# Hybrid decoder step on one core: the first norm by token rows, key steps of whole pages, the feed-forward norm at the gate

## What is computed

```python
xn = rms_norm(x, norm_mix)                                  # x * rsqrt(mean(x*x) + eps) * gain
q_m,k_m,v_m,o_m,if_pre,q_a,k_a,v_a,g_m,g_a = split(xn @ w_in)
h_m = mlstm_chunkwise(...)                                  # 8 heads of 128, gates from if_pre
h_a = moba_attention(...)                                   # sample rows read 8 pages of 128 cached keys and values
x = x + (sigmoid(g_m) * (h_m @ w_proj_m) + sigmoid(g_a) * (h_a @ w_proj_a)) @ w_out
x = x + cross_attend(rms_norm(x, norm_xattn), memory)  # ends in @ w_xo
xf = rms_norm(x, norm_ffn)
x = x + (silu(xf @ w_ffn_gate) * (xf @ w_ffn_up)) @ w_ffn_down      # 5632 wide
y = rms_norm(x, norm_final)
```

## Time and profile before

| | us |
|---|---|
| median of 3 runs | 2252.89 |
| lowest to highest | 2250.77 to 2255.76 |
| the profiled execution | 2252.39 |
| its span | 2250.8 |
| PE busy in the span | 2122.3 |
| DVE busy | 1206.2 |
| ACT busy | 797.4 |
| POOL busy | 63.5 |

### The profile page before, as it was taken

One profiled execution on the slowest core, in us unless ns is written; L12 is line 12 of the kernel. 1 busy time (PEld: TensorE's weight loads), 2 busy tenths in 40 slices (PEclk: granted clock), 3 DMA queues, 4 the chain that ended last, 5 costly groups with the idle time before them and its releaser, 6 DMA issues.

```text
span 2250.8 us, 40554 instructions
## 1 busy us (share of the span) xinstructions
PE 2122.3 (94%) x16438; PEld 2001.4 (89%) x16438; DVE 1206.2 (54%) x1424; ACT 797.4 (35%) x1010; POOL 63.5 (3%) x85
## 2 busy tenths in 40 slices
PE   4999998999899999999999787999999999999997
PEld 3999897899677878999998666999999999999997
DVE  3354565343555646667455446666654466566444
ACT  3333342243333333333344323333333333333333
POOL 0001011111000000000000000000000000000000
PEclk8899997999999999999999988999999999999998
DMA  7146434445588687556444351545445554554553
GB/s 247 38 150 189 131 98 157 132 152 175 169 287 309 242 307 272 158 174 216 167 141 159 131 187 59 165 154 181 149 141 173 172 182 154 164 172 138 173 159 114
DMA packets 305493, 384.82 MB, mean 171 GB/s; under 512 B 6146, under 2 KB 278690, under 8 KB 304626
## 3 DMA queue, kind: packets, MB, share of 16 engines
q1 hardware_dynamic: 300530, 365.72, 49.4%
q0 software_dynamic: 4896, 18.13, 2.5%
HBM read 370.94 MB, written 12.88 MB: 171 GB/s over the span
## 4 chain that ended last, share of the span: by engine, by line
PE 89%; DVE 5%; ACT 2%; issue 1%; SPq 1%; DMA 1%; POOL 0%; PEldq 0%; DVEq 0%; PEld 0%; ACTq 0%; POOLq 0%
PE bank L1713 19%; PE bank L1714 19%; PE bank L1717 18%; PE bank L1727 8%; PE bank L1731 6%; PE bank L2174 4%; PE bank L2173 4%; PE bank L2178 4%; PE bank L1724 1%; PE bank L1953 1%; PE bank L1952 1%; PE bank L1956 1%; DVE w_lo L1051 1%; DVE n_tmp L1083 1%; ACT w_hi L639 1%
## 5 line engine op out<-in xcount | busy, mean ns | idle before, releaser
L1051 DVE TENSOR_TENSOR w_lo<-raw,w_hi 128x2048 fp32r<-128x2048 f32 (+2 forms) x289 | 604.8, 2096 | 584.5 <-ACT w_hi L639 580.1
L1713 PE MATMUL bank<-xn_hi,w_hi 128*128 128x288 f32 x3152 | 875.0, 304 | 45.0 <-DVE xn_lo L1091 26.0
L1714 PE MATMUL bank<-xn_lo,w_hi 128*128 128x288 f32 x3152 | 867.0, 301 | 0.0
L639 ACT ACTIVATE w_hi<-raw 128x2048 fp32r<-128x2048 f32 (+2 forms) x289 | 504.2, 1746 | 687.3 <-PE bank L1717 471.8
L1713 PEld LDWEIGHTS bank<-xn_hi,w_hi 128*128 128x128 f32 x3152 | 608.4, 193 | 58.3 <-issue 41.6
L1714 PEld LDWEIGHTS bank<-xn_lo,w_hi 128*128 128x128 f32 x3152 | 608.3, 193 | 0.1
L1717 PE MATMUL bank<-xn_hi,w_lo 128*128 128x288 f32 x3152 | 450.7, 295 | 0.0
L1717 PEld LDWEIGHTS bank<-xn_hi,w_lo 128*128 128x128 f32 x3152 | 430.1, 189 | 0.0
L2173 PE MATMUL bank<-f_hi,w_hi 128*128 128x288 f32 x704 | 191.4, 296 | 0.0
L2174 PE MATMUL bank<-f_lo,w_hi 128*128 128x288 f32 x704 | 190.8, 297 | 0.0
L2173 PEld LDWEIGHTS bank<-f_hi,w_hi 128*128 128x128 f32 x704 | 132.5, 188 | 0.1
(11 more groups left out here) (363 smaller groups left out, 1764.6 us busy)
## 6 DMA issues: line engine op xcount, KB each, us to landing
raw<-w_in_dram SPq DMA_DIRECT2D x44, 2048.0 KB, 8.6
raw<-w_ffn_gate_dram SPq DMA_DIRECT2D x22, 2048.0 KB, 8.0
raw<-w_ffn_up_dram SPq DMA_DIRECT2D x22, 2048.0 KB, 8.0
raw<-w_ffn_down_dram SPq DMA_DIRECT2D x32, 1408.0 KB, 6.4
raw<-cache_k_dram SPq DMA_DIRECT2D x64, 512.0 KB, 5.3
raw<-cache_v_dram SPq DMA_DIRECT2D x64, 512.0 KB, 5.2
raw<-w_out_dram SPq DMA_DIRECT2D x8, 2048.0 KB, 8.1
w_pm_raw<-w_proj_m_dram SPq DMA_DIRECT2D x8, 1024.0 KB, 5.1
```

The costliest lines, as they stand in the source:

```text
L639: nc.scalar.activation(like(wh[ph.half(c)], src), src, ACT.Copy).then_inc(hi_ready, 1)
L1051: nc.vector.tensor_tensor(like(wl[ph.half(c)], src), src, like(wh[ph.half(c)], src).bitcast(F32), ALU.subtract).then_inc(slot_read[ph.slot ...
L1713: mm(out, wh[half][:, k, :], rh[:, k, 0:n], start=k == 0, stop=False)
L1714: mm(out, wh[half][:, k, :], rl[:, k, 0:n], start=False, stop=False)
```

## The change

Three parts.

1. The head. SP loads x into buffers of its own (`xrow0`, `xrow1`), the parameters are loaded from ACT's queue, and the main projection's first weights follow the gate weights at once. The sums of squares are taken from the rows as loaded, one token a partition: the first 128 tokens and the 32 sample tokens by ACT (a square with a running sum), the other 128 by DVE. The root then has three columns. It is put on the diagonals of three matrices (`xdiag`), and PE multiplies each block of rows by them instead of transposing: the product is the transposed block, already scaled. ACT takes it with the gain as the high half, DVE the low half, block by block through six banks, and the gate tile's products follow five blocks behind (`gate_k`). The plain transposes for `xT` and the gate steps go between the eight tiles of the first pass (`first_step`), and so does everything that copies them.
2. Key steps are whole pages: eight transposes into two banks, ACT copies one and DVE the other, then eight scores of the page before. Two pairs of buffers are used in turn (`KTb`, `KTb2`). The copy of the last batch's rows (`rows_in`) goes ahead of the pages.
3. The feed-forward norm. As each block of x is added up, ACT and DVE split x times gain, with no root. POOL squares the blocks and adds them into `fsum`; PE sums over features behind the first gate tile. The root is applied where the gate is read: DVE multiplies the gate tile by it on its way out of PSUM (`up_scale`), ACT takes the exponential of that, and after the sigmoid DVE multiplies by the root once more, for the up half.

Semaphores of the last norm are merged into one. The core of the diff:

```diff
@@ SP
+            xp = a["x_prompt"].rearrange("b (t p) d -> (b t) p d", p=P)
+            for t in range(2):
+                sp.dma_start(xrow0[:, t, :], xp[t]).then_inc(x_in[t], 16)
+                if not t:
+                    sp.dma_start(blob[:], a["blob"]).then_inc(const_in, 16)
+            sp.dma_start(xrow1[:], a["x_sample"].rearrange("b t d -> (b t) d")).then_inc(x_in[2], 16)
...
-            for n, name in enumerate(("norm_mix", "norm_xattn", "norm_mem", "norm_ffn")):
-                sp.dma_start(grow[16 * n:16 * n + 16, :], a[name].rearrange("l (k p) -> (l k) p", p=P)).then_inc(params_in, 16)
...
-            sp.wait_ge(m_zero, 1)
-            for t in range(TS):
-                sp.dma_start(m0tok[t:NS:TS, 2, :], a["state_m"][0]).then_inc(params_in, 16)
@@ POOL
+            for m in range(KT):
+                gp.wait_ge(c_xo, m + 1)
+                pc.run(nc.gpsimd.tensor_tensor(fsq[:, m % 2, :] if m else fsum[:], xT[:, m, :], xT[:, m, :], ALU.mult))
+                if m:
+                    pc.sync()
+                    pc.run(nc.gpsimd.tensor_tensor(fsum[:], fsum[:], fsq[:, m % 2, :], ALU.add))
@@ ACT, after the parameter loads (nine, then four behind m_zero)
+            act.wait_ge(x0_step, 1)
+            act.wait_ge(x_in[0], 16)
+            nc.scalar.activation(xsq[0][:], xrow0[:, 0, :], ACT.Square, accum_out=xss[:, 0:1]).then_inc(x0_step, 1)
+            act.wait_ge(x_in[2], 16)
+            nc.scalar.activation(xsq[2][0:NS], xrow1[:], ACT.Square, accum_out=xss[0:NS, 2:3]).then_inc(x0_step, 1)
+            act.wait_ge(x0_step, 1 + x0_ms)
+            nc.scalar.activation(xu[:], xms[:], ACT.Ln).then_inc(x0_step, 1)
+            act.wait_ge(x0_step, 1 + x0_ln)
+            nc.scalar.activation(xr[:], xu[:], ACT.Exp, scale=-0.5).then_inc(x0_step, 1)
+            hi(p_gate, 0, 0, 0, gate_src)
+            act.wait_ge(gains_set, 2)
+            for k in range(KT):
+                act.wait_ge(x0_mm, k + 1)
+                nc.scalar.activation(xh[:, k, :], B[2 + k % 6][:, 0:NT], ACT.Copy, scale=gains[:, k:k + 1]).then_inc(x0_hi, 1)
@@ ACT and DVE, key copies
+                for n in range(PAGES):
+                    act.wait_ge(d_tr, b * 16 + (2 * n + 1))
+                    act.wait_ge(d_ss, b * PAGES + (n + 1))
+                    a_copy((KTb, KTb2)[n % 2][0][:], B[2 + 2 * (n % 2)][:].rearrange("p (h c) -> p h c", c=P)).then_inc(d_kta, 1)
@@ ACT, feed-forward
+            def xg_hi(c):
+                for k in range(4 * c, 4 * c + 4):
+                    act.wait_ge(c_xo, k + 1)
+                    nc.scalar.activation(xh[:, k, :], xT[:, k, :], ACT.Copy, scale=gains[:, 48 + k:49 + k]).then_inc(nh_ready, 1)
...
             def up_evac(f, i, t):
-                act.wait_ge(gemm_done, ph.conv(i, t + 1))
-                a_copy(fg[:, t, :], G[ph.bank(t)][:, 0:NT])
-                nc.scalar.activation(fe[:, t, :], G[ph.bank(t)][:, 0:NT], ACT.Exp, scale=-1.0).then_inc(evac_done[ph.bank(t)], 1)
+                act.wait_ge(f_g, i * 2 + (t + 1 + f * FH))
+                nc.scalar.activation(fe[:, t, :], fg[:, t, :], ACT.Exp, scale=-1.0).then_inc(f_e, 1)
@@ DVE, head
+            nc.vector.tensor_tensor_reduce(out=xsq[1][:], in0=xrow0[:, 1, :], in1=xrow0[:, 1, :], scale=1.0, scalar=0.0,
+                                           op0=ALU.mult, op1=ALU.add, accum_out=xss[:, 1:2]).then_inc(x0_step, 1)
+            dve.wait_ge(gains_t, 1)
...
+            nc.vector.tensor_tensor(xdiag[:], ident.unsqueeze(1).broadcast_to([P, 3, P]), xr[:].unsqueeze(2).broadcast_to([P, 3, P]),
+                                    ALU.mult).then_inc(x0_step, 1)
+            for k in range(KT):
+                dve.wait_ge(x0_mm, k + 1)
+                dve.wait_ge(x0_hi, k + 1)
+                nc.vector.scalar_tensor_tensor(xl[:, k, :], B[2 + k % 6][:, 0:NT], gains[:, k:k + 1], xh[:, k, :].bitcast(F32),
+                                               ALU.mult, ALU.subtract).then_inc(x0_lo, 1)
+                if k == 7:
+                    lo(p_gate, 0, 0, 0, gate_src)
@@ DVE, feed-forward
+                    dve.wait_ge(nh_ready, 4 * 2 + k + 1)
+                    last = nc.vector.scalar_tensor_tensor(xl[:, k, :], xT[:, k, :], gains[:, 48 + k:49 + k], xh[:, k, :].bitcast(F32),
+                                                          ALU.mult, ALU.subtract)
...
+            def up_scale(f, i, t):
+                dve.wait_ge(gemm_done, p_up[f].conv(i, t + 1))
+                nc.vector.tensor_tensor(fg[:, t, :], G[p_up[f].bank(t)][:, 0:NT], fr[:], ALU.mult).then_inc(f_g, 1)
+                nc.vector.engine_nop().then_inc(evac_done[p_up[f].bank(t)], 1)
...
+                dc.run(nc.vector.tensor_tensor(fg[:, t, :], fg[:, t, :], fr[:], ALU.mult))
...
+                    if j >= 2:
+                        up_scale(f, i, j - 2)
@@ PE, head
+            for k in range(KT):
+                out = B[2 + k % 6]
+                if k >= 6:
+                    pe.wait_ge(x0_lo, k - 5)
+                for t in range(2):
+                    one(out[:, t * P:(t + 1) * P], xrow0[:, t, k * P:(k + 1) * P], xdiag[:, t, :])
+                one(out[:, TP:NT], xrow1[:, k * P:(k + 1) * P], xdiag[0:NS, 2, 0:NS]).then_inc(x0_mm, 1)
+                if k >= 5:
+                    gate_k(k - 5)
...
+                for s in ((), (0,), (1, 2), (3, 4), (5,), (6,), (7, 8), ())[j]:
+                    x_tiles(s)
@@ PE, key steps
+                for n in range(PAGES + 1):
+                    if n == 1:
+                        pe.wait_ge(d_h, b + 1)
+                    if n < PAGES:
...
+                        for h in range(H):
+                            c = n % 2 * H * DH + h * DH
+                            last = tr(B[2 + 2 * (n % 2) + h // 4][:, h % 4 * P:(h % 4 + 1) * P], ring(n // 2)[:, c:c + DH])
+                            if h % 4 == 3:
+                                last.then_inc(d_tr, 1)
...
+                        for h in range(H):
+                            m = h % GROUPS
                             last = one(B[6 + page // 4][m * NS:(m + 1) * NS, (page % 4) * P:(page % 4 + 1) * P],
+                                       qpad[:, h * NS:(h + 1) * NS], kt[h // 4][:, m, :], start=h < GROUPS, stop=h >= GROUPS)
@@ PE, feed-forward
-            pe.wait_ge(c_xo, 4)
-            norm(3, NT)
+            pe.wait_ge(c_xo, 12)
...
+                    if not j and not f:
+                        pe.wait_ge(sq_ready, KT // 2 * 2 + 1)
+                        mm(B[2][:, 0:NT], ones[:], fsum[:], start=True, stop=True).then_inc(sq_used, 1)
```

More of the change, by code:

```diff
@@ L238, in build @@
         top[0] = free0
-        first_scratch = norm_scratch(0, ("sq", "tmp", "ms", "r", "u"))
+        xrow0 = put("x_p_rows", [P, 2, D])
+        xdiag = put("x_diag", [P, 3, P])
+        xss, xms, xr, xu = [put(f"x_{n}", [P, 3]) for n in ("ss", "ms", "r", "u_")]
+        assert top[0] <= ha0
+        xrow1 = at("x_s_rows", [NS, D], xT_at)
+        xsq = [at(f"x_sq{t}", [P, D], xn_at + t * 4 * D) for t in range(3)]
         top[0] = ha0
@@ L289, in build @@
         DP = put("d_P", [P, PAST + NS])
+        KTb2 = [at(f"d_KT2{n}", [P, 4, P], dp_at + n * 4 * 4 * P) for n in range(2)]
         PT = at("d_PT", [P, PAGES, P], dp_at)
@@ L341, in build @@
         fg, fe, fa = [put(f"f_{n}", [P, 2, NT]) for n in ("g", "e", "a")]
+        fr, fms, fu, fsum = [put(f"f_{n}", [P, NT]) for n in ("r", "ms", "u", "sum")]
+        fsq = put("f_sq", [P, 2, NT])
         assert top[0] <= nc.sbuf_usable_end
@@ L736, in ml_body @@
                             ml_evac(i, j - 2)
+                        if not attn:
+                            first_step(j)
                     if attn:
@@ L994, in up_body @@
                 for j in range(4):
-                    if j or f or not first:
+                    if j > 1 or f or not first:
                         hi(p_up[f], i, j // 2, j, src256(p_up[f].slot(j // 2), j % 2))
@@ L1270, in ml_body @@
                 for j in range(8):
+                    if gemm and not attn:
+                        first_step(j)
                     if gemm:
@@ new lines, in gate_k @@
+            def gate_k(k):
+                half, out = p_gate.half(0), G[p_gate.bank(0)][:, 0:NT]
+                pe.wait_ge(x0_lo, k + 1)
+                if k == 0:
+                    pe.wait_ge(hi_ready, 1)
+                mm(out, wh[half][:, k, :], xh[:, k, :], start=k == 0, stop=False)
+                mm(out, wh[half][:, k, :], xl[:, k, :], start=False, stop=False)
+            for k in range(KT):
[7 more added lines that the diff above has]
+                    gate_k(k - 5)
@@ new lines, in _, with x_tiles @@
+            for k in range(KT - 5, KT):
+                gate_k(k)
+            pe.wait_ge(slot_read[2], 1)
+            for k in range(KT):
+                last = mm(G[p_gate.bank(0)][:, 0:NT], wl[p_gate.half(0)][:, k, :], xh[:, k, :], start=False, stop=k == KT - 1)
+            last.then_inc(gemm_done, 1)
+            def x_tiles(s):
```

(4 more changed lines are left out.)

399 lines of the change are left out of this document (218 added, 181 removed).

## The result

The changed kernel takes 2218.89 us (median of 4 runs, 2217.04 to 2224.43) beside 2251.83 for the kernel before (2247.33 to 2255.76): 0.986 of the time, with an interval from 0.983 to 0.989. That is 33 us less where 60 were forecast, a gain clear of the scatter, but outside the range (2174 to 2214). The profiled execution took 2218.0 us, of which 2216.2 are its span.

The account below looks back on a forecast made before the run. The prediction took PE as the bound, busy 2122 of 2250.8 us. Head 24, pages 20 and feed-forward norm 16 sum to 60 us, so 2252.4 - 60 = 2192 us, range 2174 to 2214.

Parts of the forecast that it names:

- 16 x 0.72 = 11.5: Head: PE multiplies 16 blocks by the diagonals at 0.72 us each, priced from the norm's sum, part at half clock.
- Its last sentence: Head: a first weight tile past 50 us with ACT on time would mean a low clock and a mis-sized head term.
- 49 if it stays at half: Head: upper bound in us for the first weight tile, forecast at 41.3, if the clock stays at half.
- Head, what was moved: Head: transposes and gate steps moved between the first eight tiles cost that group 5.1 us more; parameter loads on ACT hide.
- rival A: Head: ACT's parameter loads are held behind SP's big loads, losing 7 to 14 us, total taken as 2203; chance 0.25.
- Paged steps: Paged stage: a page takes 1.63 us instead of 1.88, saving 2.5 us in each of eight batches, 20 us.
- Rival C: Paged stage: pages save nothing because the pauses grow with the block, total 2212 us; chance 0.08.
- Feed-forward norm: Norm before the feed-forward part: POOL's sum of squares comes late, excluding DVE's steps; gain 16 us, bounds 12 to 27.
- T + 14.3: Feed-forward norm: forecast end of the first gate tile, in us after T, the end of the third w_xo quarter.
- Rival B: Feed-forward norm: POOL and DVE do not hinder each other with short steps, gain 27 us, total 2181; chance 0.12.
- Feed-forward loop: Gate loop: DVE's extra scaling, 1.8 us more in 25.6, costs no time.
- D: Gate loop: DVE becomes late, costing 44 times its overrun; from 1.4 us on 2254 us and more; chance 0.03.

Follow-up runs that it names:

- e2_warm: The changed kernel with 73 idle products on PE ahead of the multiplication by the diagonals in the head: 2202.1 us, 0.979 of the kernel before.
- e5_act_squares: The changed kernel with the feed-forward norm's squares on ACT in place of POOL, which keeps the 15 sums: 2211.82 us, 0.983 of the kernel before.
- e7_after_again: The changed kernel itself, unchanged, timed and traced once more: 2210.94 us, 0.979 of the kernel before.
- e1_old_head: The changed kernel with the head of the kernel before, keeping the new page steps and feed-forward norm: 2213.65 us, 0.983 of the kernel before.

## Why the prediction was wrong

**Head, the clock: the step that failed.** "16 x 0.72 = 11.5" took the price of a block from a row in which the clock was partly high, and so set 19.7 us for the stage from the first block to the first weight tile. With PE at the low clock until 59.5 us the stage took 38.2, at the high one 22.0 (e2_warm): 16.2 us are the clock. Its last sentence named the case: a first tile past 50 with ACT on time means the clock. I should have taken the low level as likely, since the old head ran at it too (in the trace of before a product of the gate takes 0.24 us from 56.68 to 60.28).

**Head, the weights.** The row behind 0.72 has one product of 288 columns; a block has three, of 128, 128 and 32, each with its own two weight loads. So a block costs 1.72 at the low and 0.97 at the high clock, and the stage lies over the prediction's own bounds at either level: 38.2 where "49 if it stays at half" leaves 49 - 21.6 = 27.4, and 22.0 where 36 leaves 14.4. The account: the first weight tile came at 60.64 and not 41.3, 19.3 later, of which 0.9 is a later start of the blocks, 16.2 the clock, and 2.3 what the stage costs beyond 19.7 even at the high clock (4 for the blocks, less some 1.7 for the gate's products, which cost less than the 0.19 taken). The eight tiles gave back 0.8.

**Head, what was moved.** The first weight tile to the eighth tile's end takes 58.7 us where it took 54.4: 4.3 more, 5.1 forecast. ACT's thirteen loads were issued by 9 us and the squares started at 10.36 and 16.00, so rival A is out.

**Paged steps.** Right, in the page (1.59, 1.63), the batch (2.43 less, 2.5) and the sum (20.2, 20). Rival C is out.

**Feed-forward norm.** Right in kind: POOL's sums are what PE meets last, and its chain and DVE's steps exclude each other, 31.7 us in all. But POOL's sum is not PE's longest wait there, as the prediction had it: that is 3.80 us for DVE's drawn-out splits, and 1.10 for the sum. The first gate tile ended at T + 22.7 and not T + 14.3, because of those splits and a low clock behind the wait; with less work on POOL (e5_act_squares) only 2.4 us are gained. The size came out better (19.7, 16), since the second tile follows at T + 24.2. The prediction's own sum says as much: 30.6 to 32.9 us from T - 8.1 on end at T + 22.5 to 24.8, not at T + 26, and POOL's last sum ended at T + 23.7. Rival B is out: POOL and DVE do hold each other up.

**Feed-forward loop.** Right: +0.3 us over the whole loop; D is out.

**Stages behind the change: the term that was missing.** The sum held them constant; they took 10.3 us more in the first trace and 20.2 in that of e7_after_again (13.1 up to the paged stage, 7.1 behind it), most of it PE busy for longer with the same records, at the low clock. The ledger closes: 5.3 + 20.2 + 19.7 - 3.7 - 6.6 - 0.3 = 34.6, the difference of the two spans.

So two thirds of the gain that was expected of the head are lost to the clock in the head itself (16.2 of 24), and what is left of it is given back to the clock in the first pass in the two traces of this kernel. The old head does about as well (e1_old_head). That the second timing of the changed kernel, 2210.94 us, lies inside the range is luck and no support for the working: its head, too, was at the low level until 41 us.

## What to carry over

Price a 32-bit product by its weight loads and at the clock level that its place will have. In the heads here that began without idle products that was the low level, and idle products ahead of the work, in time that PE would only wait, brought the first weight tile forward by 16.6 us against the first trace of after and by 8.4 against the second. To transpose and scale, scale on another engine and transpose plainly: half of the records. Where long stretches run at a mean clock under 0.9, as the first pass here, a forecast needs some 13 us of range for work that the change doesn't touch (289.6 to 302.9 here).

## What the chip showed unexpectedly

- PE, busy without a gap for 18 and for 37 us in two executions of one program, stayed at the low clock level in that time; with dense idle products ahead it stood at the high one from the first block and kept it through the same products. The Trainium skill (TensorE: Matmul & The Clock Gate, Part 1: The HAM clock gate) ties the high level to sustained activity; a busy PE in the profile's sense wasn't enough here.
- Two traces of one program differ by 9.5 us in a stretch in which no engine waits longer; the time that PE worked at the low level (58.9 and 80.4 us) accounts for it.
- POOL and DVE exclude each other with DVE first as well: a POOL step of 0.66 us takes 2.72 to 2.74 where a low half is running, three times in the trace of after. The Trainium skill (SBUF — State Buffer, Who interferes with whom) says that whichever starts first holds the other off; the prediction had only places with POOL first, and these agree for DVE first.
